# One kernel of two networks on one core: own homes for the first modulation chunks, their order against the first norm and the parameters, and early loads across a block border

## The chip, the cores and the metric

The kernel runs on one core of a Trainium2 chip. The metric is the device time of one execution, in microseconds (us), as the median of several executions. Lower is better.

## The reference

Two small networks run one after the other on 256 tokens of width 1024, in float32. The first has two layers with a modulation; the second has two more layers of another kind (the third and the fourth layer of the whole). What matters here is how the first layer begins:

```python
for l in range(DEPTH):
    mod = jax.nn.silu(c) @ w_mod[l] + b_mod[l]          # w_mod[l]: 1024 x 6144
    modc = jax.nn.silu(c_ctx) @ w_mod[l] + b_mod[l]
    sh1, sc1, gt1, sh2, sc2, gt2 = jnp.split(mod[:, None, :], N_MOD, axis=-1)
    h = rms_norm(xl, g_pre_mix[l]) * (1.0 + sc1) + sh1   # x: 256 tokens
    hc = rms_norm(xc, g_pre_mix[l]) * (1.0 + csc1) + csh1 # ctx: 256 tokens
    y, yc = token_mixer(h, hc, ...)                       # h @ w_in[l], conv, pool, attention
    ...
# second network, layer 0
proj = rms_norm_2(x, norm_mix) @ w_in
```

`token_mixer` multiplies h by the columns of `w_in`: a pooled branch, a gated convolution of 31 taps, queries, keys and values with a rotation by position, attention whose two maps are subtracted with a factor lambda, `lambda = exp(sum(lam_q1*lam_k1)) - exp(sum(lam_q2*lam_k2)) + const`.

## The kernel before, in words

The program has two blocks, `block1` (two layers) and `block2` (two layers), each with a hand-written instruction stream per engine: PE (matmul), ACT, DVE, POOL and SP. All engines meet at a barrier at the border of the blocks. SP only issues DMAs.

Weights come in tiles of 128 x 1024 float32 (512 KB). `T.load` puts each on a list of chunks, and SP issues them in that order (`load_chunks`, L1854). A tile lands in one of the `raw` slots (three in block1, five in block2) or, for modulation weights, in one of the two slots of `G`. ACT then makes the high half of each raw tile (L303) and DVE the low half (L306), and a product takes three matmuls, L317, L318 and L319. A raw slot is free again when its low half is made. SP waits for that before it issues the next load, and all loads that stand behind wait too.

**The start.** The first two groups of the modulation (shift and scale of layer 0) take 16 chunks of `w_mod`. Each chunk is four groups of small matmuls at L844 (`mod_pe`), and they go in turn through three raw slots and the two slots of G; SP waits for `pe_done` before it fills a slot again. Between them SP issues 21 small DMAs of parameters (L1887), for both layers. x and ctx (1 MB each) follow behind the last chunk, then the first three tiles of `w_in`. POOL issues the eight lambda vectors, each sent to 128 partitions, the rotation tables and the pool's counts. When all 16 chunks are summed, ACT copies the row sums (`MR`, L915), PE turns parameters (L1166) and sums (L901), and DVE makes `mod` (L937) and `gain` (L946).

**The first norm** then runs over four tiles of 128 tokens. ACT squares a tile (L425), POOL makes `rstd` (L414, L417), DVE scales it (`by_rstd`, L444), PE transposes it in eight matmuls (L638), ACT and DVE apply gain and shift to four columns each (`highs` L402, `right_columns` L404), ACT writes the high half HH (L436), DVE the low half HL (L457). `seam_act` and `seam_dve` set the order of these. `half_by_half` (L1039) then multiplies three pool tiles with tokens 0 to 255, which needs norm tiles 0 and 1 only, and again with tokens 256 to 511. Only behind it do the products for the next modulation groups run, on which SP waits with the loads behind them.

**Later places.** DVE adds up the lambda products first of all, and ACT takes their `Exp` behind the first norm (L1397). Attention of layer 0 begins with the score matmuls (L1278), the row extremes on DVE (L1730) and `Exp` on ACT (L1447); just ahead of them PE makes the mixed pool groups (L1257) and ACT copies those (L1429). At the head of block2 ACT squares the memory tokens (L595), DVE scales them (L616), PE transposes (L638), and ACT and DVE write HH (L588) and HL (L609) behind the splits of the first two weight tiles.

## Time and profile before

| | |
|---|---|
| median of 3 runs | 2321.98 us (2316.38 to 2323.59) |
| profiled execution, its own time | 2323.58 us |
| its span in the trace | 2321.8 us |
| PE, DVE, ACT, POOL busy | 2200.8, 1427.2, 889.6, 172.4 us |
| DMA | 320.78 MB, 138 GB/s in the mean |

The span runs from the first to the last instruction in the trace. "PEclk" is the clock that the throttle granted TensorE, 1.00 for 2.4 GHz and 0.50 for 1.2 GHz. A row of the timeline is a group of like instructions that follow one another, with the start of the first, their time together, and in brackets how long the engine was idle before and what ended that.

### The profile page before, as it was taken

The numbers are of one execution on the slowest core, as the hardware profiler recorded it, in microseconds if no ns is written. First come the engines' busy times: TensorE is split into PE (matmuls) and PEld (weight loads), VectorE is DVE, ScalarE is ACT, GpSimd is POOL, SyncE is SP. The second block draws the span as 40 slices with busy tenths as digits, with TensorE's granted clock in tenths as the row PEclk, the third lists the DMA queues.
The fourth block names the chain that finished last, engine by engine and source line by source line (L and its number), as shares of the span: only waits on it lengthen the run. The fifth ranks groups of instructions, "written<-read, shape, count | busy, mean of one in ns | idle before, by whom it ended". The sixth has DMA issues, their size and how long they took to land. (4 is left out here: it accounts for less than half of the span.)

```text
span 2321.8 us, 32572 instructions
## 1 busy us (share of the span) xinstructions
PE 2200.8 (95%) x12954; PEld 1874.1 (81%) x12954; DVE 1427.2 (61%) x2094; ACT 889.6 (38%) x1390; POOL 172.4 (7%) x241
## 2 busy tenths in 40 slices
PE   4999999999999999999999898999899999998998
PEld 2777767777888887788886897997788898897996
DVE  2387675664467766237967666864685565465664
ACT  2322274332342212135327444443544443344443
POOL 2412100000010000004310000000100000000000
PEclk8999999999999999999999998999989999999999
DMA  8454301233326566334421564765732566543663
GB/s 262 125 144 134 106 24 55 82 91 98 120 82 180 166 184 205 104 114 133 126 73 30 148 182 142 230 207 177 182 110 87 168 188 186 148 133 92 190 198 119
DMA packets 428705, 320.78 MB, mean 138 GB/s; under 512 B 25858, under 2 KB 379772, under 8 KB 428556
## 3 DMA queue, kind: packets, MB, share of 16 engines
q1 hardware_dynamic: 426156, 310.77, 45.1%
q0 software_dynamic: 2368, 7.93, 1.1%
q8 instruction: 104, 1.70, 0.3%
q14 instruction: 45, 0.37, 0.0%
q10 hardware_dynamic: 32, 0.01, 0.0%
HBM read 317.62 MB, written 1.05 MB: 137 GB/s over the span
## 5 line engine op out<-in xcount | busy, mean ns | idle before, releaser
L306 DVE TENSOR_TENSOR split<-raw,split 128x1024 fp32r<-128x1024 f32 x500 | 595.9, 1197 | 504.7 <-ACT split L303 500.0
L317 PE MATMUL PS<-HH,split 128*128 128x256 f32 (+1 forms) x2552 | 828.3, 325 | 39.9 <-DVE split L306 18.7
L318 PE MATMUL PS<-HL,split 128*128 128x256 f32 (+1 forms) x2552 | 815.1, 319 | 0.0
L319 PE MATMUL PS<-HH,split 128*128 128x256 f32 (+1 forms) x2552 | 813.5, 319 | 0.0
L303 ACT ACTIVATE split<-raw 128x1024 fp32r<-128x1024 f32 x500 | 507.0, 1026 | 462.8 <-PE PS L319 387.6
L317 PEld LDWEIGHTS PS<-HH,split 128*128 128x128 f32 x2552 | 489.8, 192 | 89.4 <-DVE split L306 23.1
L318 PEld LDWEIGHTS PS<-HL,split 128*128 128x128 f32 x2552 | 489.8, 192 | 36.1 <-issue 0.7
L319 PEld LDWEIGHTS PS<-HH,split 128*128 128x128 f32 x2552 | 489.3, 192 | 36.5
L317 PE MATMUL PS<-split,UH 128*128 128x512 f32 x416 | 167.4, 402 | 1.4 <-DVE split L306 1.4
L319 PE MATMUL PS<-split,UL 128*128 128x512 f32 x416 | 164.9, 396 | 0.0
L318 PE MATMUL PS<-split,UH 128*128 128x512 f32 x416 | 164.9, 396 | 0.0
L1080 ACT ACTIVATE UT<-PS 128x256 f32<-128x256 f32 (+1 forms) x88 | 38.5, 438 | 318.4 <-PE PS L319 318.4
L1650 DVE SCALAR_TENSOR_TENSOR CV<-UP,cols,CV 128x512 f32<-128x512 f32 (+1 forms) x240 | 153.7, 703 | 0.2
L892 DVE SCALAR_TENSOR_TENSOR XN<-G,silu_c,XN 128x1024 f32<-128x1024 f32 x70 | 87.9, 1281 | 37.5 <-ACT UT L1080 36.8
L317 PEld LDWEIGHTS PS<-split,UH 128*128 128x128 f32 x416 | 78.3, 188 | 21.7 <-DVE split L306 1.9
L318 PEld LDWEIGHTS PS<-split,UH 128*128 128x128 f32 x416 | 78.3, 188 | 20.0 <-issue 1.4
L319 PEld LDWEIGHTS PS<-split,UL 128*128 128x128 f32 x416 | 78.3, 188 | 19.1
L1482 ACT ACTIVATE TMP<-PS,cols 128x512 f32<-128x512 f32 (+1 forms) x48 | 27.9, 581 | 140.4 <-PE PS L319 140.4
L317 PE MATMUL PS<-split,HH 128*128 128x512 f32 (+2 forms) x224 | 80.1, 358 | 0.1
L318 PE MATMUL PS<-split,HH 128*128 128x512 f32 (+2 forms) x224 | 77.6, 347 | 0.0
L319 PE MATMUL PS<-split,HL 128*128 128x512 f32 (+2 forms) x224 | 77.6, 346 | 0.0
L1093 DVE TENSOR_TENSOR UT<-UT,PS 128x256 f32<-128x256 f32 (+1 forms) x88 | 42.9, 487 | 45.6 <-PE PS L319 41.5
(287 smaller groups left out, 2564.7 us busy)
## 6 DMA issues: line engine op xcount, KB each, us to landing
raw<-in_w_in_dram SPq DMA_DIRECT2D x120, 512.0 KB, 4.5
raw<-in_w_ffn_in_dram SPq DMA_DIRECT2D x88, 512.0 KB, 5.0
raw<-in_l_w_gate_up_dram SPq DMA_DIRECT2D x88, 512.0 KB, 3.9
G<-in_w_mod_dram SPq DMA_DIRECT2D x86, 512.0 KB, 4.0
raw<-in_w_ffn_out_dram SPq DMA_DIRECT2D x44, 512.0 KB, 3.5
raw<-in_l_w_down_dram SPq DMA_DIRECT2D x44, 512.0 KB, 4.5
raw<-in_l_w_in_dram SPq DMA_DIRECT2D x28, 512.0 KB, 4.4
raw<-in_w_attn_out_dram SPq DMA_DIRECT2D x16, 512.0 KB, 4.1
```

The costliest lines, as they stand in the source:

```text
L303: eng.activation(c["high"], c["raw"], ACT.Copy).then_inc(high_done, 1)
L306: eng.tensor_tensor(c["low"], c["raw"], c["high"].bitcast(F32), ALU.subtract).then_inc(low_done, 1)
L317: pe.matmul(out, a[0], b[0], start=first, stop=False)
L318: pe.matmul(out, a[0], b[1], start=False, stop=False)
L319: return pe.matmul(out, a[1], b[0], start=False, stop=last)
L892: ins = dve.scalar_tensor_tensor(at, c["raw"][:, 0, :], s, at, ALU.mult, ALU.add)
L1080: read_out(act.activation(tmp[:, 0, j % 2, 0:n], bank(key)[:, 0:n], ACT.Silu), key)
L1093: read_out(dve.tensor_tensor(value, tmp[:, 0, j % 2, 0:n], bank(key)[:, 0:n], ALU.mult), key)
L1482: read_out(act.activation(SG[:, done % 2, 0:n], bank(key)[:, 0:n], ACT.Sigmoid, bias=cols[:, l, 0, c:c + 1]), key)
L1650: ins = dve.scalar_tensor_tensor(CV[:, j, 0:ns, :], src, wt, CV[:, j, 0:ns, :], ALU.mult, ALU.add)
```

## The change

It does the following.

- The modulation chunks 2 to 15 of the start get a home of their own, `FIRST`, 14 chunks in the room that queries, keys and values fill later. SP issues them as seven DMAs of 1 MB without a wait. x stands behind the second of these, ctx behind the fourth, and the first three tiles of `w_in` behind the last.
- The parameters of both layers' modulation and of layer 0 go on ACT's queue, six DMAs ahead of the `Silu` and six behind. Those of layer 1, the swaps, the rotation table, the counts and the lambda vectors go on POOL's queue behind its four `rstd`.
- Squares, `rstd`, scaling and transposes of the norm no longer wait for the gain. PE transposes tiles 0 and 1 behind chunk 9, tile 2 behind chunk 13, and tile 3 inside `half_by_half`. The columns of all four tiles follow the gain at once, with one weight split between two tiles.
- The lambda sums move on DVE behind four steps of the convolution, their `Exp` on ACT behind the copies of V, ahead of the mixed groups. The turned parameters of layer 1 follow pool tile 3.
- The three raw slots of block1 are also the first three of block2's five. At the end of block1 SP loads the first three tiles of the third layer's `w_in` into them.
- The semaphores of the rotations of block2 become one for each layer, with the same order of counting.

```diff
     def weight_rings(b):
-        return ([sb("raw%d_%d" % (b, i), [P, SLOT]) for i in range(RAW[b])],
+        kept = rings[0][0] if b else []
+        place[0] += 4 * SLOT * len(kept)
+        return (kept + [sb("raw%d_%d" % (b, i), [P, SLOT]) for i in range(len(kept), RAW[b])],
...
     def mod_pe(T, pe, phase, point):
...
-        i, w = T.load(rows(A["w_mod"][l], k, 1, sec * D, D), (1, D), split=False,
-                      ring="raw" if phase == "start" and q % (RAW[0] + MOD_RING) < RAW[0] else "mod")
+        if phase == "start" and q >= MOD_RING:
+            pe.wait_ge(S("first_mod%d" % (q // 2)), 16)
+            i, w = None, FIRST[:, q - MOD_RING:q - MOD_RING + 1, :]
+        else:
+            i, w = T.load(rows(A["w_mod"][l], k, 1, sec * D, D), (1, D), split=False, ring="mod")
...
     # PE
         for q in range(KT * len(phases["start"])):
             mod_pe(T, pe, "start", q)
-        turn_params(stage_mod, ("cols", 2, 0), PARAM_LOADS)
-        for l in range(DEPTH):
-            for m in range(2):
-                turn_params(stage[:, l, m, :], ("cols", l, m), PARAM_LOADS)
-        mod_turn(T, pe, phases["start"][-1])
-        pe.wait_ge(S("swaps_loaded"), 16)
+            if q == 3:
+                turn_params(stage_mod, ("cols", 2, 0), 0)
+                for m in range(2):
+                    turn_params(stage[0][:, m, :], ("cols", 0, m), 0)
+            if q == 9:
+                norm_pe(T, pe, "L0_n1", [0, 1, 2, 3], 0, 2)
+            elif q == 13:
+                norm_pe(T, pe, "L0_n1", [0, 1, 2, 3], 2, 3)
+        mod_turn(T, pe, phases["start"][-1], FIRST_TURN)
...
     # ACT
+        ready = x_ready(0, 0)
+        for t in range(4):
+            ready(act, t)
+            square(act, "L0_n1", t, t)
+            if t == 1:
+                mod_act(act, "start", KT - 1)
+        mod_act(act, "start", 2 * KT - 1)
+        act.wait_ge(S("L0_gains"), 1)
+        for t in range(4):
+            highs(act, "L0_n1", t, HF, ...)
+            if t < 3:
+                split_until(act, ("turn",) + phases["start"][-1], t + 1)
...
+            if l == 0:
+                for m in range(DEPTH):
+                    act.wait_ge(S("lam_sums"), m + 1)
+                    act.activation(lams[:, m, 2:4], lams[:, m, 0:2], ACT.Exp).then_inc(S("lam_exps"), 1)
             for g in range(4):
                 key = (L + "mixed", g)
...
     # SP
+    EARLY = [rows(A["l0_w_in_2"], 0, KT, COL_QI + j * P, P) for j in range(RAW[0])]
+
+    def load_early(sp):
+
+        for slot, piece in enumerate(EARLY):
+            c = [c for c in in_ring["raw"] if c["sem"] is slot_full["raw"][slot]][-1]
+            sp.wait_ge(low_done, c["split"] + 1)
+            sp.dma_start(view(rings[0][0][slot][:, :], (KT, P)), piece).then_inc(c["sem"], 16)
...
+        def load_first():
+            for i in range(1, KT):
+                l, sec = phases["start"][2 * i // KT]
+                sp.dma_start(FIRST[:, 2 * i - 2:2 * i, :], rows(A["w_mod"][l], 2 * i % KT, 2, sec * D, D)).then_inc(S("first_mod%d" % i), 16)
+                if i == 2:
+                    sp.dma_start(X[:, 0:2, :], ...).then_inc(S("x_loaded"), 16)
+                if i == 4:
+                    sp.dma_start(X[:, 2:4, :], ...).then_inc(S("ctx_loaded"), 16)
+
+        load_chunks(sp, 0, {MOD_RING: load_first})
+        load_early(sp)
```

**SP's queue, from its head.** Before, the last chunk and what follows it (each DMA of a `raw` slot waits for PE):

```order
L1872 DMA raw_2_63<-in_w_mod_dram 128x1024 [waits pe_done]
L1872 DMA G<-in_w_mod_dram 128x1024 [waits pe_done] x2
L1872 DMA raw_0_61<-in_w_mod_dram 128x1024 [waits pe_done]
L1880 DMA X<-in_x_dram 128x2x1024
L1881 DMA X<-in_ctx_dram 128x2x1024
L1872 DMA raw_1_62<-in_w_in_dram 128x8x128 [waits pe_done]
```

Now, from the second instruction on:

```order
L1939 DMA G<-in_w_mod_dram 128x1024 x2
L1949 DMA first_mod<-in_w_mod_dram 128x2x1024 x2
L1951 DMA X<-in_x_dram 128x2x1024
L1949 DMA first_mod<-in_w_mod_dram 128x2x1024 x2
L1953 DMA X<-in_ctx_dram 128x2x1024
L1949 DMA first_mod<-in_w_mod_dram 128x2x1024 x3
L1939 DMA raw_0_61<-in_w_in_dram 128x8x128
```

x and ctx have moved ahead of ten and six chunks, and no DMA down to the first tiles of `w_in` waits.

**PE, from chunk 12 to the first product.** Now (before, the transposes of all tiles stand behind the last turn at L901):

```order
L850 MATMUL PS<-first_mod,silu_c 32x256 [waits first_mod6]
L641 MATMUL PS<-ident,XN 128x128 [waits bank_read1,L0_n1_xn]
L641 MATMUL PS<-ident,XN 128x128 [waits bank_read2]
L850 MATMUL PS<-first_mod,silu_c 32x256 [waits first_mod7]
L908 MATMUL PS<-ident,MR 128x128 [waits bank_read3,bank_read7]
L320 MATMUL PS<-HH,split_0_64 128x256 [waits bank_read3,low_done,L0_n1_parts]
```

The rows between them are further matmuls of the same chunk or tile. The first product stands right behind the turn of the last sums, and what it waits for are columns alone.

**ACT behind the last sums.** Now (before, L425 stands behind the gain and between the tiles):

```order
L428 ACTIVATE XN,ss<-X 128x1024 [waits x_loaded] x2
L922 ACTIVATE MR<-PS 128x256 [waits pe_done]
L428 ACTIVATE XN,ss<-X 128x1024 [waits pe_done,ctx_loaded] x2
L922 ACTIVATE MR<-PS 128x256 [waits pe_done]
L405 ACTIVATE TMP<-PS,mod,gain 128x128 [waits pe_done,L0_gains]
L439 ACTIVATE HH<-TMP 128x4x128 [waits bank_read4]
L439 ACTIVATE HH<-TMP 128x4x128 [waits bank_read5]
L306 ACTIVATE split_0_64<-raw_0_61 128x1024 [waits slot_full0]
L405 ACTIVATE TMP<-PS,mod,gain 128x128 [waits pe_done,L0_n1_parts]
```

The four squares are gone from between gain and columns, and a split now stands between two tiles.

## Rows read from the trace of the kernel before

**Rows 1.** The page: PE busy in tenths, in 40 slices of the span.
```profile
PE   4999999999999999999999898999899999998998
```
**Rows 2.** Stretches: length, then busy (count) of each engine, PEclk, DMA share, GB/s.
```profile
40.00:50.00 10.00, 3.65 (x16) 3.28 (x16) 6.83 (x14) 6.78 (x14) 1.83 (x4) 0.50 0.94 276
0.00:10.00 10.00, 2.46 (x21) 0.66 (x25) 0.00 (x0) 1.47 (x2) 9.47 (x19) 1.00 0.78 213
14.00:18.00 4.00, 2.16 (x16) 0.40 (x16) 1.11 (x5) 0.00 (x0) 0.00 (x0) 1.00 1.03 397
30.00:40.00 10.00, 4.57 (x47) 1.40 (x39) 0.93 (x5) 3.42 (x10) 1.10 (x3) 0.94 1.01 363
```
**Rows 3.** Timeline of the start: start, time together, what, and what ended the idle.
```profile
3.12 0.54 POOL L1516 DMA_DIRECT2D TMP<-in_lam_k_dram  x1
5.69 1.08 PE L844 MATMUL PS<-raw,silu_c 128*32 128x256 f32 x8 [0.59 <-DMA raw<-in_w_mod_dram]
34.81 0.64 PE L844 MATMUL PS<-raw,silu_c 128*32 128x256 f32 x8 [1.03 <-DMA raw<-in_w_mod_dram]
35.52 0.38 ACT L915 ACTIVATE MR<-PS 128x256 f32<-128x256 f32 x1 [10.62 <-PE PS L844]
36.64 0.37 DVE L946 SCALAR_TENSOR_TENSOR gain<-mod,cols 128x8 f32<-128x8 f32 x2
40.53 3.65 PE L638 MATMUL PS<-ident,XN 128*128 128x128 f32 x16 [4.14 <-DVE XN L444]
41.75 1.06 ACT L303 ACTIVATE split<-raw 128x1024 fp32r<-128x1024 f32 x1 [2.15 <-DMA raw<-in_w_in_dram]
42.71 1.49 ACT L402 ACTIVATE TMP<-PS,mod,gain 128x128 f32<-128x128 f32 x4
42.84 1.22 DVE L306 TENSOR_TENSOR split<-raw,split 128x1024 fp32r<-128x1024 f32 x1 [0.85 <-ACT split L303]
43.98 1.36 DVE L404 TENSOR_SCALAR TMP<-PS,gain,mod 128x128 f32<-128x128 f32 x4
44.24 0.63 ACT L436 ACTIVATE HH<-TMP 128x512 fp32r<-128x512 f32 x1
45.26 1.47 DVE L457 TENSOR_TENSOR HL<-TMP,HH 128x512 fp32r<-128x512 f32 x2
51.61 0.58 PE L317 MATMUL PS<-HH,split 128*128 128x256 f32 x1 [7.43 <-DVE HL L457]
```
**Rows 4.** DMA issues of the first 60 us: count, KB each, median us to landing.
```profile
TMP<-in_inv_counts_dram POOLq DMA_DIRECT2D x1, 512.0 KB, 9.2
TMP<-in_lam_q_dram POOLq DMA_DIRECT2D x4, 32.0 KB, 6.7
```
**Rows 5.** Timeline behind the first products.
```profile
60.09 1.04 PE L638 MATMUL PS<-ident,XN 128*128 128x128 f32 x8
64.34 0.39 PE L317 MATMUL PS<-HH,split 128*128 128x256 f32 x1 [0.41 <-DVE HL L457]
84.96 0.80 PE L317 MATMUL PS<-HH,split 128*128 128x512 f32 x1 [4.58 <-DVE split L306]
156.67 1.23 DVE L306 TENSOR_TENSOR split<-raw,split 128x1024 fp32r<-128x1024 f32 x1 [2.09 <-ACT split L303]
```
**Rows 6.** Timeline where attention of layer 0 begins.
```profile
294.13 1.28 ACT L1447 ACT_TABLE_LOAD   x1
294.59 1.22 DVE L1730 TENSOR_REDUCE mx<-PS 128x2 f32<-128x1024 f32 x1 [8.74 <-PE PS L1278]
```
**Rows 7.** Timeline of the head of block2.
```profile
1636.29 1.06 ACT L303 ACTIVATE split<-raw 128x1024 fp32r<-128x1024 f32 x1 [1.83 <-DMA raw<-in_l_w_in_dram]
1639.19 1.23 DVE L306 TENSOR_TENSOR split<-raw,split 128x1024 fp32r<-128x1024 f32 x1 [0.43 <-ACT split L303]
1643.17 0.55 PE L317 MATMUL PS<-HH,split 128*128 128x256 f32 x1 [3.52 <-DVE HL L609]
```

More of the change, by code:

```diff
@@ L1189, in _ @@
             if skip:
-                half_by_half(T, pe, L + "n1", tiles, lambda p: (L + "pool", p), lambda p: rows(w_in, 0, KT, COL_P + p * P, P))
+                half_by_half(T, pe, L + "n1", tiles, lambda p: (L + "pool", p), lambda p: rows(w_in, 0, KT, COL_P + p * P, P), 3)
             else:
@@ L1200, in _ @@
                 mod_pe(T, pe, L + "proj", j)
+                if j == 3 and l == 0:
+                    for m in range(2):
+                        turn_params(stage[1][:, m, :], ("cols", 1, m), 1)
                 if j < 2 and first == 2:
@@ L1375, in _, with copy_params @@
                                 ACT.Silu), ("c",))
+        load_params(param_loads(0)[6:])
         now["hold"] = True
-        for q in range(KT * len(phases["start"])):
-            mod_act(act, "start", q)
-        now["hold"] = False
-        now["hold"] = True
-        for l, m in ((2, 0), (0, 0), (0, 1), (1, 0), (1, 1)):
+        def copy_params(l, m):
             key = ("cols", l, m)
@@ L1390, in _ @@
             if l == 0:
-                act.wait_ge(S(L + "gains"), 1)
-                seam_act(act, L + "n1", tiles, HF, lambda k, t: gain[:, 0, 0, k, t // 2:t // 2 + 1],
-                         lambda k, t: mod[:, 0, SHIFT_1, k, t // 2:t // 2 + 1], x_ready(0, 0), lead=("turn",) + phases["start"][-1])
-            if l == 0:
-                for m in range(DEPTH):
-                    act.wait_ge(S("lam_sums"), m + 1)
-                    act.activation(lams[:, m, 2:4], lams[:, m, 0:2], ACT.Exp).then_inc(S("lam_exps"), 1)
+                act.wait_ge(S("filled"), 4)
             norm_wait(act, L + "n1", [0, 1, 2, 3])
@@ L1403, in _ @@
                 mod_act(act, L + "proj", j)
+                if j == 3 and l == 0:
+                    for m in range(2):
+                        copy_params(1, m)
             for j in range(NCH):
@@ L1512, in _ @@
         pool.memset(silu_c[:], 0.0).then_inc(S("silu_zeroed"), 1)
-        pool.memset(TMP[:, 0:512], 0.0).then_inc(S("zeroed"), 1)
-        for l in range(DEPTH):
-            for m, v in enumerate(("lam_q1", "lam_k1", "lam_q2", "lam_k2")):
-                pool.dma_start(lamv[:, l, m, :], A[v][l:l + 1, :].broadcast_to([P, 64])).then_inc(S("lam_loaded"), 16)
-        pool.dma_start(swaps[:], A["swaps"]).then_inc(S("swaps_loaded"), 16)
+        for one in stage:
+            pool.memset(one[:, :, :], 0.0).then_inc(S("zeroed"), 1)
+        pool.memset(half[:], -0.5).then_inc(S("filled"), 1)
         pool.memset(ones[:], 1.0).then_inc(S("filled"), 1)
-        pool.memset(half[:], -0.5).then_inc(S("filled"), 1)
         pool.memset(UP[:], 0.0).then_inc(S("filled"), 1)
@@ L1603, in _ @@
-        wait_read(dve, ("cols", 1, 0))
-        dve.wait_ge(S("filled"), 4)
+        now["hold"] = True
+        ready = x_ready(0, 0)
+        for t in range(4):
+            ready(dve, t)
+            by_rstd(dve, "L0_n1", t)
+            if t == 2:
+                wait_read(dve, ("cols", 2, 0))
+                wait_read(dve, ("cols", 0, 0))
+                wait_read(dve, ("cols", 0, 1))
+                mod_columns(dve, phases["start"][0])
+        mod_columns(dve, phases["start"][1])
+        wait_read(dve, ("turn",) + phases["start"][-1])
@@ new lines, in _, with lambda_sums @@
+        dve.wait_ge(S("L0_gains"), 1)
+        for t in range(4):
+            right_columns(dve, "L0_n1", t, HF, lambda k, t: gain[:, 0, 0, k, t // 2:t // 2 + 1],
+                          lambda k, t: mod[:, 0, SHIFT_1, k, t // 2:t // 2 + 1])
+            lows(dve, "L0_n1", t, HF)
+            if t < 3:
+                split_until(dve, ("turn",) + phases["start"][-1], t + 1)
+        now["hold"] = False
+        dve.wait_ge(S("filled"), 4)
+        def lambda_sums():
+            dve.wait_ge(S("lam_loaded"), 16 * 8)
+            for m in range(DEPTH):
+                wait_read(dve, ("cols", 1, m))
+            for l in range(DEPTH):
+                for m in range(2):
+                    dve_link(dve, dve.tensor_tensor(lamv[:, l, 2 * m, :], lamv[:, l, 2 * m, :], lamv[:, l, 2 * m + 1, :], ALU.mult))
+                dve.tensor_reduce(lams[:, l, 0:2], lamv[:, l, 0:4:2, :], AX_X, ALU.add).then_inc(S("lam_sums"), 1)
@@ L2503, in _ @@
     def _(sp):
-        load_chunks(sp, now["chunk0"])
+        load_chunks(sp, now["chunk0"] + len(EARLY))
         for t in range(2):
```

111 lines of the change are left out of this document (54 added, 57 removed).

## The prediction

> **What bounds the kernel now.** I read the page first. PE is busy at 9 tenths or more in nearly every slice, so a stage is worth only what PE waits there; the first slice has 4 [rows 1]. The change touches the first 75 us, the start of the first attention and the border of the blocks, so I went to these in the stretches and the timeline.
>
> The start is a line with two parts. The first is a load: in the first ten microseconds the DMA engines are busy for 0.78 of the time, so from about 2.2 us on, and then at 0.94 to 1.03 until past 40 us, with 213 GB/s in the first ten and 397 and 363 later [rows 2]; PE waits at the modulation chunks for their landing, 0.59 us at 5.69 and 1.03 at 34.81 [rows 3]. The second begins where the last chunk has landed. It is summed, ACT copies the sums at 35.52, the gain is there at 37.01, and only then come squares, scaling and transposes; the first product starts at 51.61 [rows 3]. In these 14.6 us PE does 3.65 us of transposes. It is at the 1.2 GHz level in 40 to 50 us [rows 2]. Later there is a hole of 4.58 us at 80.4 [rows 5].
>
> **The change, part by part.**
>
> *The second part of the line.* Squares, rstd, scaling and transposes of tiles 0 to 2 need x and ctx alone, and these now stand ahead of ten and six chunks in SP's queue, so they are over while the last chunks land. Behind the gain there stay, from the row durations of rows 3: columns of tile 0 on ACT 1.49 beside 1.36 on DVE; HH until 2.1 and 2.7; HL, 0.74 for each half, until 3.6. ACT splits the first weight tile from 2.7 to 3.8 and DVE makes its low half until 5.0; this split was done between the tiles before, too. Tile 1: columns on ACT 3.8 to 5.3, on DVE 5.0 to 6.4, HH, and the two HL until 7.9. The first product therefore starts 7.9 us behind the gain and not 14.6: **6.7 us** less.
>
> *The first part.* Ahead of the last pair of chunks SP has 16 chunks of 0.524 MB, x and ctx with 2.10 and the identity with 0.07: 10.56 MB. ACT's parameters add 0.15. POOL's counts, 0.52, are issued behind the last rstd, near 28 us, and travel beside the last pairs: 11.2 MB in all. The rotation table, the swaps, the lambda vectors and the second set of parameters come later. Nothing in SP's queue waits for PE any more. The best stretch of large rows shows 397 GB/s, the stretch with x, ctx and tiles of w_in 363 [rows 2]. I take 370, since the first microseconds are never the best: 2.2 + 30.3 = 32.5 us for the landing of the last pair, against 34.81. At 397 it is 30.4. The other end is the pace of before: 16 chunks with the parameters, vectors, swaps, table and counts were 9.98 MB by 34.81, which is 306 GB/s, and 11.2 MB at that pace land at 38.8.
>
> From the landing PE has two chunks, not one, 1.28 us at the faster row (0.64) and 2.16 at the slower (1.08) [rows 3]. With 0.07 to ACT's copy, and 1.49 from there to the end of the gain as now, the gain is ready at 32.5 + 2.84 = 35.3 and the first product starts at 43.2 in place of 51.61: **8.4 us** earlier in all, of which 1.7 come from the load.
>
> *half_by_half.* Between its three products stood the transposes of tiles 2 and 3, 1.04 us each [rows 5]. Tile 2 is now turned earlier; tile 3 stays, with the 4.25 us from its transposes to the second half (60.09 to 64.34) and the wait of 0.41. **1.0 us** less.
>
> *Moved issues.* Six parameter DMAs now stand ahead of ACT's Silu. At POOL's 0.54 us for an issue [rows 3] and with a table load of 1.28 [rows 6] the Silu ends by about 6.2 us; the first chunk landed at 5.69, and PE waits again for every later one, so this costs nothing. PE waits for all twelve of ACT's DMAs behind chunk 3, and twelve chunks' products, three tiles' transposes and the sums are queued behind that. The nearest row, 32 KB of POOL under a full SP queue, lands in 6.7 us, the counts in 9.2 [rows 4]. Issued by 8.5, the parameters land at 15 to 18, when PE has lost some 4 us; it makes them up, as a pair needs 1.3 to 2.2 us of PE and about 2.8 of DMA. POOL now issues 20 DMAs between the last rstd and its first pooling; at 0.54 each they end near 39 us, and pool tile 0 is ready some 20 us later. DVE's lambda sums, six instructions at about 0.25 each (two of the gain's take 0.37 [rows 3]), fall into the stretch where it has 2.09 us of idle ahead of a split [rows 5]; if that were not so, PE would wait for 1 us.
>
> *The first attention.* ACT now loads the Exp table, 1.28 us [rows 6], and does two Exp on two columns, 1.6 us with them, ahead of the four mixed copies. The first scores use the banks of the last two of these. The table load at 294.13 goes, but it was hidden: the first Exp waited for DVE's extremes at 294.59 [rows 6]. These now wait for scores that wait for copies. I take **1.0 us more**, between 0 and 1.6.
>
> *The block border.* ACT waits 1.83 us for the first tile [rows 7], which looks like the gain. But DVE scales both norm tiles first, and its own wait for a split is 0.43; HL and PE's 3.52 us of idle hang on DVE [rows 7]. **0.4 us** less, between 0 and 1.8 (all of ACT's wait).
>
> Sum: 8.4 + 1.0 - 1.0 + 0.4 = 8.8 us. Against the profiled execution, 2323.58, that is 2314.8; against the median of the three runs, which is 1.6 lower, 2313.2. I give 2314.0. What a measurement of this kernel can tell from no change is about 0.3%, 7 us.
>
> **The rivals.**
>
> *The load does not get faster.* For it: the DMA share is near 1 before, and by 306 GB/s the last pair lands at 38.8, the first product starts at 49.5 and the sum falls to 2.5; at 330 GB/s to 5.3. Against it: share 1.0 went with 213 as with 397 GB/s, and the slow stretch held the small transfers of the lambda vectors, which now come later. Time: 2318.5 to 2321. The Trainium skill's page "DMA: Bandwidth & Descriptors", section "Issuing engines are not separate DMA queues", speaks for this rival: transfers started by several engines run on the same 16 DMA engines, and spreading them saves the issue alone. By that rule moving the parameters to ACT gains nothing, and what remains is that the vectors are later.
>
> *PE stays at the lower level.* Its work is short and spread between landings. Then the pair ahead of the last, landed at 29.7, takes 2.2, tile 2's transposes 1.8 (16 matmuls took 3.65 [rows 3]), and the last pair 2.2, until 35.9. The gain comes at 37.8 and the first product at 45.7: the sum is 6.3, the time 2316.5 to 2317.3. Against it: before, with less work for PE, the chunk at 34.81 took 0.64 [rows 3].
>
> *The parameters land late, and the kernel is slower.* PE has 13.6 us of work between them and ACT's last copy of the sums: 12 chunks at 0.64, 24 transposes at 0.13, two turns, and 2 us for the lower level at the start. Add 1.5 to the gain and 7.9 to the product. The point from which it decides is a landing at 29 us: there nothing is won. At 34 us the kernel is 5 us slower, 2328.6. For it: twelve small transfers on a second queue, one of 124 short rows, beside a queue that is always full. Against it: 6.7 and 9.2 us in rows 4.
>
> *The later hole closes too.* The 4.58 us at 80.4 come from a tile load that SP may issue only when the first chunk behind `half_by_half` is multiplied. The order around it is the same now, so I expect the hole again. If it closed, 2309.4.
>
> *The border does nothing.* It is in the range of its term; it would not be seen in the time.
>
> **How the numbers follow.** The forecast 0.56, its own range 2311 to 2317.5 (landing 30.4 to 34.5 and the ends of the small terms). The load no faster 0.18, PE at the lower level 0.12, parameters late 0.07, hole closed 0.07. Four fifths of the forecast, 0.45, and the closed hole, 0.07, are faster by over 0.3%: 0.52. The rest of the forecast, 0.11, the slow load and the lower level are within: 0.41. Slower: 0.07. The range 2309.5 to 2321.0 leaves out the late parameters and the outer parts of the slow load and of the closed hole.
>
> **What would show it.** The last pair's products near 32.5 us, the first product (L320) near 43.2 with no square or transpose behind the gain, the second half 11.7 us behind it, and a hole of 4 to 5 us near 71. The row extremes of the first attention (294.59 before) should start 8.4 us earlier, 1.0 less than the 9.4 of the products ahead of them. At the head of block2 DVE's second low half should start without a wait, and PE's idle ahead of the first product fall from 3.52 to about 3.1. The forecast is wrong if the gain comes after 38 us, if PE waits long behind chunk 3, or if the time between 100 and 290 us grows by more than 1 us.

## The result, and the profile after

The changed kernel takes **2308.78 us** (median of 5 runs, 2303.22 to 2312.03), the kernel before 2323.59 on the same chip (5 runs, 2316.38 to 2327.60): a ratio of **0.9937, 95% interval 0.9921 to 0.9953**. That is 14.8 us less where 8.8 were forecast, and a time just under the range's low end of 2309.5. The profiled execution took 2303.22 us, the shortest of its five; so what it shows has to be checked against other executions, and most of the runs below do that.

The page of the changed kernel, the span and the rows of 40 slices that answer to [rows 1]:

```profile
span 2301.4 us, 32565 instructions
...
PE   5999999999999999998999898999899999998998
...
PEclk8999999999999999999999999999989999999999
```

PE's row differs from that of before in two digits: the first is 5 in place of 4, and one in the middle 8 in place of 9. The stretches that answer to [rows 2] (length, then busy time of each engine, granted clock, DMA share, GB/s):

```profile
0.00:10.00 10.00, 2.26 (x17) 0.58 (x17) 0.00 (x0) 1.47 (x2) 4.79 (x11) 1.00 0.81 266
10.00:20.00 10.00, 4.40 (x35) 1.88 (x39) 0.00 (x0) 1.96 (x6) 0.02 (x1) 1.00 1.03 392
34.00:42.00 8.00, 0.44 (x2) 0.20 (x2) 6.31 (x16) 6.32 (x14) 5.18 (x10) 0.57 1.10 326
```

The first ten microseconds move 266 GB/s and not 213, and the next ten 392. From 34 to 42 us PE has two transposes to do and its granted clock falls to the lower of its two levels, 1.2 GHz (0.57 in the mean of these 8 us, 0.50 in the 2 us behind them). The timeline of PE over the start, against [rows 3] and [rows 5] (start, time together, what, idle before and what ended it):

```profile
17.53 0.90 PE L1173 MATMUL PS<-ident,TMP 128*128 128x128 f32 x3 [5.46 <-DMA TMP<-in_conv_w_dram]
18.36 3.41 PE L850 MATMUL PS<-first_mod,silu_c 128*32 128x256 f32 x32
...
32.44 1.07 PE L850 MATMUL PS<-first_mod,silu_c 128*32 128x256 f32 x16 [0.57 <-DMA first_mod<-in_w_mod_dram]
34.01 0.44 PE L908 MATMUL PS<-ident,MR 128*128 128x128 f32 x2 [0.51 <-ACT MR L922]
42.71 0.58 PE L320 MATMUL PS<-HH,split 128*128 128x256 f32 x1 [8.26 <-DVE HL L460]
...
55.40 0.39 PE L320 MATMUL PS<-HH,split 128*128 128x256 f32 x1 [0.41 <-DVE HL L460]
...
73.63 0.50 PE L320 MATMUL PS<-HH,split 128*128 128x512 f32 x1 [1.82 <-DVE split L309]
```

PE waits 5.46 us for the parameters, then does four chunks in a row and is level with the load again. Between the last sums and the first product stand columns and splits alone, as in ACT's and DVE's timelines:

```profile
34.70 0.37 DVE L953 SCALAR_TENSOR_TENSOR gain<-mod,cols 128x8 f32<-128x8 f32 x2
...
35.10 1.50 ACT L405 ACTIVATE TMP<-PS,mod,gain 128x128 f32<-128x128 f32 x4 [1.14 <-DVE gain L953]
...
38.64 1.48 ACT L405 ACTIVATE TMP<-PS,mod,gain 128x128 f32<-128x128 f32 x4
...
41.19 1.47 DVE L460 TENSOR_TENSOR HL<-TMP,HH 128x512 fp32r<-128x512 f32 x2
```

**Four profiles of each kernel.** The two unaltered kernels were profiled three more times each (runs e0, r1, r2 and e5, r3, r4 below). The span cut at five marks, as the means of four; behind each the four values.

| part | before | changed | less |
|---|---|---|---|
| to the first product | 52.6 (51.61, 52.68, 53.10, 53.09) | 42.6 (42.71, 41.96, 42.77, 42.93) | 10.0 |
| to the first mixed group | 236.9 (238.18, 235.56, 237.09, 236.85) | 235.3 (233.51, 234.09, 236.85, 236.76) | 1.6 |
| to the first row extremes of attention | 4.80 (all within 0.01) | 6.02 (all) | -1.2 |
| to ACT's first square of the last block | 1338.9 (1337.69, 1339.43, 1339.31, 1339.15) | 1340.1 (1336.95, 1342.83, 1340.65, 1340.04) | -1.2 |
| to that block's first product | 10.95 (10.89, 10.97, 11.14, 10.81) | 10.37 (all) | 0.6 |
| to the end of the span | 676.4 (678.6, 676.2, 676.0, 674.9) | 672.6 (671.8, 673.4, 672.3, 672.8) | 3.9 |
| sum | 2320.6 | 2307.0 | 13.6 |

The last part is the surprise: 3.9 us in a block where the prediction saw only the early load.

The first part can be cut once more, at the end of `gain` (L946 and L953). Before, it is there at 37.01, 38.93, 38.10 and 39.66 us, 38.4 in the mean, and the first product stands 14.2 us behind it (13.4 to 15.0). In the changed kernel it is there at 35.07, 34.31, 35.13 and 35.28, 34.9 in the mean, and the first product stands 7.6 us behind it in all four. So of the 10.0 us, 3.5 come ahead of the gain and 6.6 behind it (rounded).

### The profile page after: what moved, and what is told of

It is laid out like the page before. It is cut to its first block and busy times, and to the rows that moved or that the text cites. A ratio compares the mean times of both kernels' runs of the same rounds, so it can differ in the third digit from the quotient of the medians.

```text
span 2301.4 us, 32565 instructions
## 1 busy us (share of the span) xinstructions
PE 2187.0 (95%) x12954; PEld 1866.4 (81%) x12954; DVE 1428.6 (62%) x2094; ACT 887.3 (39%) x1389; POOL 176.6 (8%) x251
## 5 line engine op out<-in xcount | busy, mean ns | idle before, releaser
L321 PEld LDWEIGHTS PS<-HL,split 128*128 128x128 f32 x2552 | 488.3, 191 | 35.9 <-issue 0.7
L1087 ACT ACTIVATE UT<-PS 128x256 f32<-128x256 f32 (+1 forms) x88 | 38.4, 438 | 313.7 <-PE PS L322 313.7
L899 DVE SCALAR_TENSOR_TENSOR XN<-G,silu_c,XN 128x1024 f32<-128x1024 f32 x70 | 87.9, 1281 | 36.6 <-ACT UT L1087 35.9
```

The costliest lines, as they stand in the source:

```text
L321: pe.matmul(out, a[0], b[1], start=False, stop=False)
L899: ins = dve.scalar_tensor_tensor(at, c["raw"][:, 0, :], s, at, ALU.mult, ALU.add)
L1087: read_out(act.activation(tmp[:, 0, j % 2, 0:n], bank(key)[:, 0:n], ACT.Silu), key)
```

## The experiments

Each ran with the kernel before on the same chip; ratios are to that kernel, with 95% intervals. "Marks" are those of the table above.

### The changed kernel again (e5), the early load alone (e1)

e5 is the changed kernel unaltered. e1 is the kernel before with this alone (the shared slots go with it):

```
+        load_early(sp)
...
-        load_chunks(sp, now["chunk0"])
+        load_chunks(sp, now["chunk0"] + len(EARLY))
```

> The changed kernel once more, unaltered. Theory A (the change shortens the hole behind the halves for good, because the tile loads there find a shorter queue): the hole shows about 1.8 us again, PE stays at the 2.4 GHz level through it, and the profiled mixed groups start 13 to 14 us earlier than in the kernel before. Theory B (the short hole was chance, forecast otherwise right): a hole of 4 to 5 us, the mixed groups about 9 us earlier, and the median against the kernel before nearer to 0.9960 (9 us) than to 0.9937 (14.8 us).

> The kernel before with the early load of the third layer's first weight tiles alone. My term for it is 0.4 us less, with bounds of 0 and 1.8: DVE's second split at the head of the last block waits for nothing, PE's idle ahead of the first product falls from 3.52 to about 3.1 us, ratio 0.9998. Rival: the load was on the way to the first product for more than that, up to the whole of ACT's wait of 1.83 us and the split behind it, and the ratio is 0.9992 or below.

e5: 2310.19 us (6 runs), **0.9941 (0.9919 to 0.9963)**, so the size of the gain holds. Its hole (PE's wait for the first tile behind `half_by_half`, 4.58 us in [rows 5]) is 1.84 us and its mixed groups start at 276.05, 13.7 us earlier than in the first profile of before (289.79): theory A so far. But the clock did fall behind the hole here (0.68 in 74 to 78 us), which A did not say.

e1: 2321.31 us (12 runs), 0.9991 (0.9977 to 1.0004). DVE has its two splits in one row and PE's idle is 3.17 us where [rows 7] have 3.52:

```profile
1636.73 2.35 DVE L309 TENSOR_TENSOR split<-raw,split 128x1024 fp32r<-128x1024 f32 x2
...
1642.01 0.35 PE L320 MATMUL PS<-HH,split 128*128 128x256 f32 x1 [3.17 <-DVE HL L612]
```

From ACT's first square to the first product it takes 10.55 us and not 10.89: the term of 0.4 measures 0.3. The ratio can't tell it from the rival, whose 0.9992 it also fits; the two rows do.

### The hole closed, in both kernels (e6, e7)

The products of the first two modulation chunks of the next phase go between the halves, so that the chunk load that holds up SP's queue finds its slot free some 10 us earlier (at 54.27 us in e6, at 64.70 in the first profile of the changed kernel).

```
             if h == 0:
+                between(0)
                 norm_wait(pe, name, tiles)
...
-                half_by_half(T, pe, L + "n1", ..., 3)
+                half_by_half(T, pe, L + "n1", ..., 3,
+                             between=(lambda _: [mod_pe(T, pe, L + "proj", j) for j in range(2)]) if l == 0 else nothing)
...
-                mod_pe(T, pe, L + "proj", j)
+                if j >= 2 or l or not skip:
+                    mod_pe(T, pe, L + "proj", j)
```

> The changed kernel, with the products of the first two modulation chunks of the later groups put between the two halves of the first products, so that the next chunk's load and the tile loads queued behind it are issued about 8 us earlier. If the hole comes from that queue, it goes: 1.8 us less by the profiled execution of the changed kernel, 4 to 7 us less if the profiled one was lucky and the usual hole is 4.6 us with a fall of the clock behind it. If the load alone is late whatever its issue (bandwidth), nothing changes.

> The kernel before with the same move of two chunks' products between the halves. If the hole of 4.58 us is the late issue of a load, it goes, and with it the stretch at the 1.2 GHz level behind it (2.4 us): 5 to 7 us less, ratio 0.9970 to 0.9978, and mixed groups that start 5 to 7 us earlier. If PE's lower clock behind the hole is independent of it: 4 to 4.6 us less. If the load is late for bandwidth: no change.

e6: 2303.61 us (6 runs), 0.9910 (0.9888 to 0.9931), 6.6 us below the changed kernel on the same chip. e7: 2316.51 us (12 runs), **0.9970 (0.9955 to 0.9985)**, 7.3 below the kernel before. The hole is gone in both, and so is the fall of the clock behind it. In e6, over the stretch where the changed kernel waits:

```profile
54.00:66.00 12.00, 12.00 (x97) 11.02 (x90) 3.59 (x3) 4.64 (x6) 3.58 (x4) 1.00 0.76 220
66.00:78.00 12.00, 12.00 (x64) 8.61 (x63) 2.78 (x3) 4.82 (x7) 11.24 (x10) 1.00 0.37 99
```

PE is busy for all 24 us at a granted clock of 1.00 (2.4 GHz). From the first product to the first mixed group it now takes 229.6 us (e6) and 230.1 (e7), where the unaltered kernels take 233.5 to 238.2. So an earlier issue is enough to close the hole, and it costs 4 to 8 us, clock included, in either kernel. e6 is the first version that beats both.

### The norm behind the gain (e4), and what makes the hole long (e9, e10, e0)

e4 is the changed kernel with squares, rstd, scaling and transposes of the first norm behind the gain; homes and order of the loads stay. Its core on PE (on ACT and DVE the gain's steps move ahead of the squares in the same way):

```
-            if q == 9:
-                norm_pe(T, pe, "L0_n1", [0, 1, 2, 3], 0, 2)
-            elif q == 13:
-                norm_pe(T, pe, "L0_n1", [0, 1, 2, 3], 2, 3)
         mod_turn(T, pe, phases["start"][-1], FIRST_TURN)
+        norm_pe(T, pe, "L0_n1", [0, 1, 2, 3], 0, 3)
```

e9 is the kernel before with the load of the rotation table issued when POOL starts pooling:

```
-                pool.dma_start(grid, A["grid_rope"]).then_inc(S("grid_loaded"), 16)
...
                 wait_read(pool, (L + "pool", g))
+                if g == 0 and l == 0:
+                    pool.dma_start(grid, A["grid_rope"]).then_inc(S("grid_loaded"), 16)
```

> The changed kernel with rstd, scaling and transposes of the first norm put back behind the gain: the loads' new homes and order stay. By my terms the gain stays at 35 us and the first product comes 6.7 us later than in the changed kernel, at about 49.5; the median is 6 to 7 us over the changed kernel's, near 0.9965 of the kernel before. On the hole, theory G (the transfers start slowly when the DMA engines were without work for some 25 us before, as they were for 25 and 26 us in the two profiles with a hole of 4.5 us, and for 20 and 19 in the two with 1.8 us): here they are without work for about 27 us, so the hole is 4.5 us again and the median 2.7 to 5 us worse still, 0.998. Theory H (the new homes shorten the hole): 1.8 us.

> The kernel before with one edit: POOL issues the load of the rotation table (0.26 MB) not at the start but when it starts pooling, at about 69 us, 4 us ahead of the burst of tile loads whose slow start makes the hole. Theory G (long rest of the DMA engines makes the start slow): the first tile lands in about 5.4 us, not 8, and the hole is 1.8 to 2.5 us in place of 4.5; the start is about 0.7 us earlier by the bytes taken out of it; 3 to 5 us less in all, ratio 0.998 to 0.9985. Theory H (homes) or chance: the hole stays at 4.5 us, ratio 0.9997.

e4: 2321.26 us (12 runs), **0.9999 (0.9989 to 1.0009)**: 11 to 12 us over the changed kernel, and not the 6 to 7 I expected. The last chunks land as early as in the changed kernel, but the first product comes 10 us later. PE's timeline, with DVE's row of the gain:

```profile
32.26 1.94 PE L850 MATMUL PS<-first_mod,silu_c 128*32 128x256 f32 x16 [1.74 <-DMA first_mod<-in_w_mod_dram]
...
35.64 0.37 DVE L953 SCALAR_TENSOR_TENSOR gain<-mod,cols 128x8 f32<-128x8 f32 x2
...
44.31 1.10 PE L641 MATMUL PS<-ident,XN 128*128 128x128 f32 x8 [1.59 <-DVE XN L447]
...
52.74 0.58 PE L320 MATMUL PS<-HH,split 128*128 128x256 f32 x1 [7.33 <-DVE HL L460]
```

But e4 does not put the old order back. In it all four squares and tile 2's transposes stand ahead of the columns, and the first product comes 16.7 us behind the gain, where the kernel before takes 13.4 to 15.0. So this run does not price the new homes alone: its gain is there at 36.01, 2.4 us ahead of the mean of before, and the worse order takes 2.5 back. Against the old order the norm's new place is worth 14.2 less 7.6, 6.6 us.

Its DMA engines had rested 16 us only, since POOL's loads came late, so it could not test theory G; its hole was 1.83 us.

e9: 2318.58 us (12 runs), 0.9990 (0.9980 to 1.0000), with holes of 1.42 and 0.88 us, 2.3 in all: as G said, though the median shows less than expected. So two more runs put G to the test. e10 is e4 with POOL's loads ahead of its rstd; e0 is the kernel before, unaltered.

```
-                seam_pool(pool, L + "n1", tiles)
                 pool.dma_start(counts, A["inv_counts"]).then_inc(S("counts_loaded"), 16)
...
+                seam_pool(pool, L + "n1", tiles)
```

> The kernel of the run with the norm behind the gain, with POOL's loads (counts, second parameters, swaps, rotation table, lambda vectors) issued ahead of its rstd, as the kernel before had them, so that nothing is moved between about 48 us and the burst at 74. Theory G (a rest of about 25 us of the DMA engines makes the next burst start slowly): the burst's third and fourth microsecond fall under 200 GB/s, the first tile lands in about 8 us, the hole is 4.5 us, and the median 2 to 5 us over that of its twin, near 1.0005. Theory H (the homes of the changed kernel shorten the hole, or the order of its loads): 1.8 us as in the twin.

> The kernel before once more, unaltered: if the hole of 4.5 us with the fall of the clock behind it belongs to the kernel, it shows again, with 150 to 190 GB/s in the third or fourth microsecond of the burst; if it was chance, some other length between 1.5 and 4.5 us.

e10: 2323.71 us (10 runs), 1.0012 (1.0000 to 1.0025), with a hole of 3.01 us. e0: one run, 2321.41 us. **Theory G fell.** e0's DMA engines had rested 25 us, as long as in the profile of [rows 5], and its burst started quickly (242, 314 and 322 GB/s in the microseconds from 76.3 us on), with a hole of 2.58 us. e10's rested 20 us and it started slowly (139 GB/s from 80 to 81 us, issue at 77.4).

e10 shows something else, in one profile: with POOL's loads back ahead of the norm the last pair of chunks lands at 36.41 us and not at 32.26, and the gain is there at 39.03, no earlier than in the kernel before. It keeps the new homes, ACT's queue, and x and ctx (2.1 MB) ahead of the last chunks. So, as far as these two profiles show, what ends the load earlier in the changed kernel is that POOL's loads come behind it.

### Both kernels twice more (r1, r2, r3, r4)

> The kernel before, unaltered, a further profile. If the slow start of the burst belongs to it: first tile about 8 us behind its issue and a hole of 4.5 us. If it is chance: either 8 and 4.5, or 5.5 to 6 and 2.6. First product between 51.6 and 53.1 us; from there to the first mixed group 238 to 239 us with the slow start, 235.6 without.

> As the run ahead of it: 8 us and 4.5 if the slow start belongs to the kernel; one or the other if it is chance.

> The changed kernel, unaltered, a further profile. If the slow start is no part of it: first tile 5.4 us behind its issue, a hole of 1.8 us, 233 to 234 us from the first product (41.8 to 42.7) to the first mixed group. If it is chance, a slow start with a hole of 3.5 us or more shows here at times too.

> As the run ahead of it: 1.8 us if the slow start is no part of the changed kernel; at times 3.5 us or more if it is chance.

One execution each: 2323.19, 2321.43, 2310.74 and 2310.70 us. The slow start showed in all four: the first tile's split started 7.6 to 7.8 us behind the issue, the holes are 3.77 and 3.80 us before, 3.77 and 3.75 in the changed kernel. Stretches of one microsecond, from about 1 us behind the burst's first issue on, of the changed kernel in its first profile and then in r3:

```profile
65.70:66.70 1.00, 1.00 (x6) 0.81 (x5) 0.00 (x0) 0.00 (x0) 0.92 (x2) 1.00 0.70 164
66.70:67.70 1.00, 1.00 (x6) 0.78 (x5) 0.00 (x0) 0.00 (x0) 0.92 (x2) 1.00 0.82 270
67.70:68.70 1.00, 1.00 (x6) 0.82 (x5) 0.00 (x0) 0.00 (x0) 1.00 (x2) 1.00 1.07 335
68.70:69.70 1.00, 1.00 (x6) 0.82 (x5) 0.00 (x0) 0.00 (x0) 0.92 (x2) 1.00 1.15 348
```

```profile
64.70:65.70 1.00, 1.00 (x6) 0.81 (x5) 0.00 (x0) 0.00 (x0) 0.92 (x2) 1.00 0.56 193
65.70:66.70 1.00, 1.00 (x6) 0.82 (x5) 0.00 (x0) 0.00 (x0) 0.92 (x2) 1.00 0.74 289
66.70:67.70 1.00, 1.00 (x6) 0.77 (x6) 0.00 (x0) 0.00 (x0) 0.92 (x3) 1.00 0.47 141
67.70:68.70 1.00, 1.00 (x6) 0.82 (x5) 0.00 (x0) 0.00 (x0) 1.00 (x1) 1.00 0.63 184
```

The same program, the same engines busy with the same things, and 141 and 184 GB/s where the other execution has 335 and 348. The difference is there at the issue already. SP's row for the first tile, in the first profile and in r3:

```profile
65.07 0.43 SPq L1939 DMA_DIRECT2D raw<-in_w_in_dram  x1
...
63.93 1.73 SPq L1939 DMA_DIRECT2D raw<-in_w_in_dram  x1
```

This issue takes 1.35 to 1.99 us in all eight profiles with a slow start and 0.43 to 0.70 in the seven with a quick one. Behind the long hole PE starts at the 1.2 GHz level:

```profile
74.44 0.80 PE L320 MATMUL PS<-HH,split 128*128 128x512 f32 x1 [3.77 <-DVE split L309]
```

The slow start thus comes in either kernel, in 3 of 4 profiles before and 2 of 4 after, and costs the changed kernel about 3 us (236.8 against 233.5 and 234.1 to the first mixed group). Theory A is wrong as it was put: the change does not shorten the hole for good. Whether it makes the slow start rarer is open. With e1, x1, e2 and x2, whose start is that of one of the two kernels but for the banks, it came in 5 of 6 profiles of the old start and in 2 of 6 of the new one, and so few can't tell this from chance. What makes it slow stays open.

### The banks (x1, x2)

Both kernels give results the seven PSUM banks in turn. Two openings, those of the start's `mod_turn`, now ask for bank 3 by name (`FIRST_TURN`) and leave the turn, so every later result that takes its bank in turn is two banks behind where it was. In the orders of the two programs the first matmul of the last block's output projection reads, before and now:

```
L317 MATMUL PS<-split_2_15991,O2H 128x512 [waits bank_read4,bank_read5,low_done]
L320 MATMUL PS<-split_2_15972,O2H 128x512 [waits bank_read4,bank_read3,bank_read5,bank_read2,low_done]
```

Banks 4 and 5 hold the transposes that DVE turns into low halves just then. Before, the projection writes into these two and so waits for the last low half; now it writes into 3 and 2, and waits in 4 and 5 only for the halves that it reads first. Each edit is one line behind the last `mod_turn` of the start:

```
+        bank_no[0] += 5      # x1, in the kernel before
+        bank_no[0] += 2      # x2, in the changed kernel
```

> The kernel before, with the round of PSUM banks moved on once at the start so that every later result goes to the bank that it has in the changed kernel; nothing else is changed. If the bank decides: the first product of the last block's output projection starts 0.4 us behind the last transposes in place of 2.2, the 1.57 us of idle ahead of it are gone, the fall of the clock there shrinks, and the part from the block's first product to the end takes 672 to 673.5 us in place of 675 to 678.5; the median is 3 to 4 us below that of the kernel before, ratio 0.9985. If it is chance or another part of the change: 676 us and ratio 1.0000.

> The changed kernel with the banks of the kernel before. If the bank decides: the wait of about 1.6 us ahead of the output projection's first product is back, 675 to 678 us from the block's first product to the end, and the median 3 to 4 us over that of the changed kernel, ratio 0.9955. If not: 672.5 us and 0.9940.

PE's timeline at that place, in the changed kernel, then x2, then x1:

```profile
1763.89 0.63 PE L2249 MATMUL PS<-ident,Y 128*128 128x128 f32 x4 [0.34 <-DVE O2L L2551]
1764.28 0.48 PE L320 MATMUL PS<-split,O2H 128*128 128x512 f32 x1
```

```profile
1770.45 0.63 PE L2250 MATMUL PS<-ident,Y 128*128 128x128 f32 x4 [0.34 <-DVE O2L L2552]
1772.65 0.76 PE L320 MATMUL PS<-split,O2H 128*128 128x512 f32 x1 [1.56 <-DVE O2L L2552]
1773.21 0.63 PE L321 MATMUL PS<-split,O2H 128*128 128x512 f32 x1
```

```profile
1783.10 0.63 PE L2189 MATMUL PS<-ident,Y 128*128 128x128 f32 x4 [0.34 <-DVE O2L L2491]
1783.48 0.48 PE L317 MATMUL PS<-split,O2H 128*128 128x512 f32 x1
```

With the old banks the projection starts 2.2 us behind the last transposes, with the new ones 0.4; and behind the wait PE runs at the lower level (in x2 a granted clock of 0.51 in the 3.35 us from 1772.65, in the changed kernel 1.00). To the end of the span it takes 676.0 us in x2 and 673.9 in x1, against 672.6 and 676.4 in the table. **That the bank decides this wait is shown both ways.**

The medians are less plain. x2: 2312.60 us (12 runs), 0.9973 (0.9962 to 0.9984). That is 2.4 us over e5 and 3.8 over the first measurement of the changed kernel, on other chips; against the kernel before on its own chip it keeps 6.6 us, where those two had 13.6 and 14.8, so by the ratios the old banks cost more than 3 to 4 us. x1: 2321.00 us (12 runs), 1.0002 (0.9991 to 1.0014), where 0.9985 was expected: no gain over the kernel before. Part of the answer is the first attention, which the new banks make slower. PE's mixed groups and first scores, and DVE's first row extremes, in x1 and in x2:

```profile
291.43 3.60 PE L1258 MATMUL PS<-PP,raw 128*128 128x512 f32 x8
295.04 2.75 PE L1279 MATMUL PS<-KTT,QT 64*128 64x512 f32 x8
...
297.03 1.22 DVE L1731 TENSOR_REDUCE mx<-PS 128x2 f32<-128x1024 f32 x1 [9.55 <-PE PS L1279]
```

```profile
276.21 3.60 PE L1273 MATMUL PS<-PP,raw 128*128 128x512 f32 x8
279.73 2.36 PE L1294 MATMUL PS<-KTT,QT 64*128 64x512 f32 x8
...
281.07 1.23 DVE L1789 TENSOR_REDUCE mx<-PS 128x2 f32<-128x1024 f32 x1 [1.42 <-PE PS L1294]
```

From the mixed groups to the extremes x1 takes 5.60 us and x2 4.86, against 4.80 before and 6.02 in the changed kernel. That leaves some 2 to 3 us of x1's shortfall unexplained.

### The Exp moved (e8), and no early load (e2)

e8 is e6 with ACT's Exp on the lambda sums between the two halves of V's copies; e2 is the changed kernel without the early load.

```
-            if l == 0:
-                for m in range(DEPTH):
+                if l == 0 and nn == 0:
+                    for m in range(DEPTH):
```

```
-        load_early(sp)
...
-        load_chunks(sp, now["chunk0"] + len(EARLY))
+        load_chunks(sp, now["chunk0"])
```

> The changed kernel with the two chunks' products between the halves (hole closed) and the Exp on the lambda sums moved between the two halves of V's copies on ACT. If the Exp table load stands in the way of the first scores as I forecast, the row extremes start 1.0 to 1.2 us earlier against the products ahead of them than in the kernel with the hole closed alone: 2302.5, ratio 0.9905. If something else holds the first scores there, as in the kernel with the hole closed, 0.9910.

> The changed kernel without the early load of the last block's first three tiles (they are loaded when the block starts). My term: 0.4 us more, ratio 0.9943; the first product of the block comes 0.3 to 0.5 us later behind ACT's first square. If the slots that the blocks now share make the load wait for the splits of the block before and nothing more, the same.

e8: 2304.02 us (5 runs), 0.9930 (0.9919 to 0.9942), no better than e6. From the mixed groups to the extremes it takes 5.63 us where e6 takes 6.02: moving the table load gives back 0.4 us and not 1.0 to 1.2. x1, with the new banks and no table load there, takes 5.60, and x2, with the old banks and the table load, 4.86. So the new banks alone cost 0.8, the table load alone 0.06, and 0.4 only behind the new banks.

e2: 2309.32 us (7 runs), 0.9959 (0.9939 to 0.9979), not to be told from the changed kernel. The head of the block, in the changed kernel and in e2:

```profile
1619.19 1.06 ACT L598 ACTIVATE XN<-X 128x1024 f32<-128x1024 f32 x1 [3.54 <-PEq L1958]
...
1624.45 2.35 DVE L309 TENSOR_TENSOR split<-raw,split 128x1024 fp32r<-128x1024 f32 x2
...
1629.56 0.55 PE L320 MATMUL PS<-HH,split 128*128 128x256 f32 x1 [3.37 <-DVE HL L612]
```

```profile
1619.43 1.06 ACT L598 ACTIVATE XN<-X 128x1024 f32<-128x1024 f32 x1 [3.54 <-PEq L1957]
...
1626.35 1.23 DVE L309 TENSOR_TENSOR split<-raw,split 128x1024 fp32r<-128x1024 f32 x1 [0.44 <-ACT split L306]
...
1630.33 0.55 PE L320 MATMUL PS<-HH,split 128*128 128x256 f32 x1 [3.52 <-DVE HL L612]
```

10.37 us from square to product with the early load, 10.90 without: 0.5 us.

### Each block with its better banks (x3), beside its twin (x4)

x4 is e6 unaltered; x3 has one line more at the head of each block's PE program:

```
         mod_turn(T, pe, phases["start"][-1], FIRST_TURN)
+        bank_no[0] += 2
...
         T = Tensor(pe)
+        bank_no[0] += 5
```

> The changed kernel with the two chunks' products between the halves, the banks of the kernel before in the first block, and those of the changed kernel in the last. If each block follows its own banks: 4.8 to 4.9 us from the first mixed group to the row extremes of the first attention (6.0 in its twin), no wait ahead of the output projection's first product, 672 to 674.5 us from the last block's first product to the end, and a median about 1 us below its twin's. If the banks act in some other way, one of the two is not as said.

> Its twin, the kernel with the hole closed, once more: 6.0 us from the first mixed group to the row extremes, 229 to 230 us from the first product to the first mixed group whatever the start of the burst, and a median near 2303.6, ratio 0.991.

x3: **2301.27 us** (6 runs, 2297.59 to 2308.30), **0.9917 (0.9900 to 0.9934)**. x4: 2302.99 us (5 runs, 2298.98 to 2306.86), 0.9919 (0.9906 to 0.9933). Each block followed its own banks: in x3 4.87 us to the extremes (6.02 in x4), no wait ahead of the projection, 672.8 us to the end. The medians differ by 1.7 us, less than these runs can tell; both beat the kernel before on the same chip by 19 to 21 us, and the changed kernel on other chips by 6 to 9.

## Why the prediction was wrong

The direction and the first mechanism were right. The sum was too small by 5 to 6 us against the medians, and the first measurement lies 0.7 us under the range; the second, e5 with 2310.19, lies inside it. By the means of four profiles (13.6 for 8.8) it can be told where the sum failed: 3.9 us in the last block, put at nothing, and 1.6 at the start, where the load was mis-sized.

- **First product, 8.4 forecast, 10.0 measured.** The steps came as written: last pair at 32.44 (32.5), gain done at 35.07 (35.3), first product 7.6 us behind it (7.9), so 42.71 (43.2). The 6.7 us for the work behind the gain measure 6.6. The term that failed is the 1.7 us for the load: the gain comes 3.5 us earlier. It was subtracted from a gain at 37.01, the earliest of four draws whose mean is 38.4; the load's end varies from one execution to the next, and I read one. The first product, 51.61 in that profile, is 52.6 in the mean for the same reason.
- **The load no faster.** It did not come: the first ten microseconds went from 202 to 213 GB/s (four profiles) to 266, and the gain is earlier. The page "DMA: Bandwidth & Descriptors" of the Trainium skill, section "Issuing engines are not separate DMA queues", spoke for this rival: transfers that several engines issue share the same 16 DMA engines. e10 agrees with the page: with the parameters on ACT's queue and POOL's loads early, the gain is no earlier than before (39.03). What the rival missed is the other half, that POOL's loads come later. Its sum at 330 GB/s is 5.1 and not 5.3; nothing hangs on it.
- **PE at the lower level.** It did not come in the changed kernel: PE was at 2.4 GHz until 34 us, and the fall came behind the load, with 1.2 GHz in the first microseconds of products, as before [rows 2]. In e4, without the transposes between the chunks, it did: a granted clock of 0.50 from 30 to 36 us, and 1.94 us for the last pair in place of 1.07. Of the rival's own sum, the gain at 37.8 should be 37.5: 35.9, 0.07 and 1.49.
- **half_by_half, 1.0 forecast; 1.6 to the mixed groups.** The second half came 11.7 us behind the first product in e5, as forecast, and 12.69 in the first profile, where PE stayed at the lower level longer. Like against like, the part is 1.8 us shorter with a quick start of the burst (235.6 against 233.5 and 234.1) and 0.6 with a slow one (means 237.4 and 236.8). The term holds.
- **The hole.** The forecast that it stays was right, and the rival that it closes was wrong; its length, from 1.82 to 3.77 us in four profiles of the changed kernel, was not foreseen. My account of it was right too: e6 and e7 close it by freeing the slot earlier.
- **Moved issues, 0.** Right: 5.46 us of waiting for the parameters are made up by 26.4 us, when PE waits for a landing again (1.02 us). The parameters landed at 17.5, inside 15 to 18.
- **First attention, -1.0 forecast, -1.2 measured, for the wrong reason.** The table load alone costs 0.06 (x2; 0.07 in x3), the banks alone 0.8 (x1), and the rest comes only from both. That the number fits is luck.
- **Border, 0.4 forecast.** 0.3 in e1, 0.5 against e2, 0.6 by the means. What was missed stands just ahead of it: ACT's first square comes 2.43 us behind the start of DVE's last scaling of X, and before 1.70.
- **The step that failed by omission: the banks.** The change was read for what it computes and loads. `FIRST_TURN` was in the diff, and I costed it at nothing without saying so. It moves every later result by two banks, and takes out a wait of 1.6 us and a stretch at 1.2 GHz in the last block: 3.9 us between these profiles. Over all twelve profiles with the new banks there (671.8 to 676.3) and eight with the old ones (674.9 to 678.6) the part takes 673.5 and 676.7 us: **3.2 us**. The wait is shown by x1 and x2; that all of the 3.2 us follow from it is read from the profiles, and x1's median does not bear it out. The same shift costs the 0.8 in the first attention.

What stays open: why x1's median shows no gain; and why the long middle part (first extremes to the last block) is 1.2 us longer in the mean. 0.7 of it is that step from DVE to ACT's first square at the border; e2 has it (2.42 us) and e1 has not (1.68), so the early load isn't its cause. No run tried what is. The rest of it is smaller than the spread of 6 us among four profiles of one kernel.

## What to carry to other kernels

When results take banks or slots in turn, a change of one opening moves all that follow, to the end of the program: compare the waits of the two orders at every stage's first matmul, far from the edit too, and count the shift as a term with both signs. Take work that needs no late input off the line behind the last landing: that was worth 6.6 us here. Loads that nothing needs soon belong behind those that everything waits for: with POOL's back in front the last pair landed 4 us later (e10 against e4, one profile each). When a part of a change is taken back to price it, check that the old order comes back with it; e4's did not, and its median alone would have said that the load is worth nothing. And take the ends of a forecast from several executions; where the load bounds a stretch, one profile's time for it was 1.4 us off.

## What the runs showed of the hardware

A burst of three tile loads and two chunks into resting DMA queues starts in one of two ways. In the fourth microsecond behind the issue of the first tile it moves 316 to 331 GB/s or 105 to 207, the first tile's split starts 5.4 to 6.0 or 7.4 to 8.0 us behind that issue, and the issue itself takes SP 0.43 to 0.70 or 1.35 to 1.99 us. Both kernels show both; a rest of the DMA engines of 16 to 25 us doesn't decide it (quick after 25, slow after 20); the four executions r1 to r4, made one after the other on one chip, were all slow, and three other chips showed both ways, each under two different kernels. Whether the moment plays a part was not tried.

A wait of PE costs more than its length: behind a hole of 3.8 us the granted clock is 0.50 for 5.6 us (r3), and matmuls of 512 columns follow each other at 0.43 us in place of 0.23; closing the hole gave 6.6 and 7.3 us. Behind a hole of 1.8 us it stayed at 1.00 in one execution and fell to 0.68 for 4 us in another (e5). And where the clock falls late in the program differs from one execution to the next. The stretch of 20 us that starts 360 us behind the last block's first product, in e2 and in r3:

```profile
1990.33:2010.33 20.00, 18.28 (x124) 17.80 (x123) 8.88 (x13) 7.47 (x11) 0.00 (x0) 0.77 0.36 102
```

```profile
1996.66:2016.66 20.00, 19.27 (x148) 19.19 (x149) 10.07 (x13) 7.14 (x11) 0.00 (x0) 0.91 0.40 115
```

The same matmuls, at a mean granted clock of 0.77 and 0.91: 24 fewer done in the same time. Of 23 executions of the kernel before on one chip, the slowest (2330.36 us) had a mean granted clock of 0.967 and the fastest (2313.30 us) one of 0.975.
